# Where ScalarE, VectorE and GpSimd do their share of the SSD stages, and when the rotary tables are loaded

## The reference, cut to what matters

```python
xbc = jax.nn.silu(causal_dwconv(xbc, conv_w, conv_b))       # x, B, C of every group
cb = jnp.einsum('bclgn,bcsgn->bgcls', Cm, Bm)               # C B^T, shared by a group's 4 heads
y_diag = jnp.einsum('bgecls,bcsgep->bclgep',
                    cb[:, :, None] * jnp.exp(segsum(a_dt)), X)   # decay of every head, causal
y = y + xs * jnp.repeat(d_skip, SSD_HEAD_DIM)
y = (y * jax.nn.silu(z)).reshape(Bsz, T, SSD_GROUPS, SSD_INNER // SSD_GROUPS)
y = y * lax.rsqrt(jnp.mean(y * y, -1, keepdims=True) + EPS) # norm over a group's 256 channels
...
q = rotate_retnet(q, pos); k = rotate_retnet(k, pos) * RET_QK_DIM ** -0.5
scores = jnp.einsum('bclhd,bcshd->bhcls', q, k) * decay[None, :, None]
```

## Time and profile before

| | |
|---|---|
| median of three runs | 1806.04 us (1805.96 to 1806.24) |
| profiled execution | 1805.96 us, its span 1804.2 us (1.8 us lie outside the span) |
| PE busy | 1770.2 us, 98% of the span |
| DVE busy | 1204.9 us, 67% |
| ACT busy | 730.1 us, 40% |
| POOL busy | 16.7 us, 1% |

### The profile page before, as it was taken

How to read it: one execution, slowest core, us unless ns; L and a number is a source line. 1 busy time by engine, 2 the same in 40 slices (tenths; PEclk the granted TensorE clock), 3 DMA queues, 4 the chain that set the end, 5 groups by cost and what they waited for, 6 DMA issues and landing times.

```text
span 1804.2 us, 35149 instructions
## 1 busy us (share of the span) xinstructions
PE 1770.2 (98%) x13934; PEld 1686.2 (93%) x13934; DVE 1204.9 (67%) x1702; ACT 730.1 (40%) x1078; POOL 16.7 (1%) x58
## 2 busy tenths in 40 slices
PE   7999999999999999999999999999999999999996
PEld 7998899999999999999998888888989999999996
DVE  8788765545367877783344777777775788878323
ACT  5454441112143223222224777777774333322221
POOL 0000000000000000000000000000000000000000
PEclk9999999999999999999999999999999999999998
DMA  4322332222222322332222222221212222233221
GB/s 155 113 87 85 94 105 68 64 71 69 71 92 84 93 86 89 93 97 95 96 66 73 62 62 62 62 61 53 68 55 87 93 84 91 93 93 105 87 96 62
DMA packets 39936, 149.89 MB, mean 83 GB/s; under 512 B 4384, under 2 KB 5408, under 8 KB 39216
## 3 DMA queue, kind: packets, MB, share of 16 engines
q1 hardware_dynamic: 38672, 142.16, 25.1%
q10 hardware_dynamic: 1184, 6.60, 1.1%
HBM read 146.62 MB, written 2.13 MB: 82 GB/s over the span
## 4 chain that ended last, share of the span: by engine, by line
PE 86%; DVE 8%; ACT 3%; issue 2%; DVEq 0%; DMA 0%; ACTq 0%
PE gp L365 75%; PE small L411 4%; PE small L422 1%; DVE wlo L1121 1%; PE small L605 1%; PE small L615 1%; DVE xcv L1161 1%; DVE spb L1572 1%; PE small L464 1%; DVE gr L1161 1%; ACT lbuf L968 1%; DVE dec L1236 1%; ACT lbuf L971 0%; ACT whi L698 0%; DVE sp_lo L1596 0%
## 5 line engine op out<-in xcount | busy, mean ns | idle before, releaser
L365 PE MATMUL gp<-hn_hi,whi 128*128 128x264 f32 (+1 forms) x3216 | 662.3, 287 | 14.1 <-DVE wlo L1121 11.5
L365 PE MATMUL gp<-hn_hi,wlo 128*128 128x264 f32 (+1 forms) x3216 | 654.9, 285 | 0.0
L365 PE MATMUL gp<-hn_lo,whi 128*128 128x264 f32 (+1 forms) x3216 | 654.1, 285 | 0.0
L698 ACT ACTIVATE whi<-raw 128x1024 fp32r<-128x1024 f32 (+1 forms) x249 | 273.6, 1099 | 795.0 <-PE gp L365 794.4
L1121 DVE TENSOR_TENSOR wlo<-raw,whi 128x1024 fp32r<-128x1024 f32 (+1 forms) x249 | 317.5, 1275 | 336.5 <-ACT whi L698 336.2
L365 PEld LDWEIGHTS gp<-hn_hi,whi 128*128 128x128 f32 x3216 | 502.2, 190 | 18.9 <-DVE wlo L1121 12.0
L365 PEld LDWEIGHTS gp<-hn_lo,whi 128*128 128x128 f32 x3216 | 500.2, 189 | 0.0
L365 PEld LDWEIGHTS gp<-hn_hi,wlo 128*128 128x128 f32 x3216 | 499.4, 190 | 0.0
L365 PE MATMUL gp<-hid_lo,whi 128*128 128x264 f32 (+1 forms) x704 | 141.7, 283 | 0.0
L365 PE MATMUL gp<-hid_hi,wlo 128*128 128x264 f32 (+1 forms) x704 | 141.5, 282 | 0.0
L365 PE MATMUL gp<-hid_hi,whi 128*128 128x264 f32 (+1 forms) x704 | 141.4, 282 | 0.0
(11 more groups left out here) (234 smaller groups left out, 1732.6 us busy)
## 6 DMA issues: line engine op xcount, KB each, us to landing
raw<-in SPq DMA_DIRECT2D x217, 512.0 KB, 3.6
raw<-in SPq DMA_DIRECT2D x32, 704.0 KB, 4.1
cs_bc<-cs_scratch ACTq DMA_DIRECT2D x4, 1056.0 KB, 5.8
hT<-in SPq DMA_DIRECT2D x4, 528.0 KB, 7.5
out<-yT SPq DMA_DIRECT2D x4, 512.0 KB, 2.8
rdec<-in ACTq DMA_DIRECT2D x1, 1056.0 KB, 6.3
gw<-in SPq DMA_DIRECT2D x8, 128.0 KB, 3.4
rope<-in ACTq DMA_DIRECT2D x1, 528.0 KB, 3.7
```

Source lines behind the costliest of these rows:

```text
L365: ins = pe.matmul(gp[t.par][:, h, 0:half], wp[w.par][:, cols], rp[:, k0 + k, t0 + h * half:t0 + (h + 1) * half], start=first and k == 0 an ...
L698: act.activation(whi[w.par][:, 0:kt * P], raw[w.par][:, 0:kt * P], ACT.Copy).then_inc(hi_done, 1)
```

## The change

ACT: the Silu of B now waits for C's convolution too and is done with it in one instruction, ahead of those of x and z. The Ln and Exp of the norm (steps 6 and 7, now one step) come behind the stage's first `split_hi` and no longer around it. The decays of heads 2 and 3 come in slot 3, no longer in slot 4. DVE: `split_lo` comes ahead of the first two `args`; the other two `args` move from slot 3 to slot 2, ahead of `weigh_pair(g, 0)`, which itself goes to slot 3; the convolutions of tiles 2 and 3 move one slot back, to slots 4 and 5. POOL: the mask is put on each of the four `dec[h]`, behind the exponential, in place of the one `cbs`. The two tables lie elsewhere in memory, and ACT issues their loads in slot 7 of head 0 behind the last group's `norm_out`, where it issued them in slot 5 behind the last group's products.

```diff
             def ssd_silu(g):
-                act.wait_ge(conv_done, 4 * g + 3)
-                act.activation(xcv[:, 2, :], xcv[:, 2, :], ACT.Silu)
+                act.wait_ge(conv_done, 4 * (g + 1))
+                act.activation(xcv[:, 2:4, :], xcv[:, 2:4, :], ACT.Silu)
+                wait_count(act, ysum_done, g)
+                act.activation(xs[:], xcv[:, 0:2, :], ACT.Silu)
                 act.wait_ge(pair_free[(T_SSD + 4) % 2], (T_SSD + 4) // 2 + 1 + 3 * g)
                 act.activation(zc[:, 0, :], zc[:, 0, :], ACT.Silu)
-                wait_count(act, ysum_done, g)
-                act.activation(xs[:], xcv[:, 0:2, :], ACT.Silu)
-                act.wait_ge(conv_done, 4 * g + 4)
-                act.activation(xcv[:, 3, :], xcv[:, 3, :], ACT.Silu)
...
-                if step == 4:
+                if step == 3:
                     for h in range(2, 4):
                         decay(g, h)
...
-                if step == 7:
                     act.wait_ge(yln_done, g + 1)
                     act.activation(acc[:], acc[:], ACT.Exp, scale=-0.5).then_inc(yrs_done, 1)
...
             for c in range(8):          # ACT, retention head 0
...
-                if c == 5:
-
-                    act.wait_ge(y_done, 2 * SSD_GROUPS)
+                if c == 7:
+
+                    act.wait_ge(yout_done, SSD_GROUPS)
                     act.dma_start(rope[:], ...).then_inc(tab_in, 16)
                     act.dma_start(rdec[:], dec_h).then_inc(tab_in, 16)
...
             def weigh_pair(g, c):
-                    ve.wait_ge(e_done, HPG * g + h + 1)
-                    ve.wait_ge(cbm_done, g + 1)
+                    ve.wait_ge(es_done, HPG * g + h + 1)
+                    ve.wait_ge(cbs_done, g + 1)
...
                 if c == 0:              # DVE, ssd_slot
                     tile(-1)
+                    split_lo(w)
                     args(g, 0)
                     args(g, 1)
-                    split_lo(w)
...
                     conv_(1)
+                    args(g, 2)
+                    args(g, 3)
+                elif c == 3:
                     weigh_pair(g, 0)
-                elif c == 3:
                     split_lo(w)
                     tile(2)
-                    args(g, 2)
-                    args(g, 3)
-                    conv_(2)
                 elif c == 4:
                     split_lo(w)
                     weigh_pair(g, 1)
                     tile(3)
                     take(g, 0)
-                    conv_(3)
+                    conv_(2)
                 elif c == 5:
                     take(g, 1)
                     split_lo(w)
                     add_pair(g)
                     tile(4)
+                    conv_(3)
...
             with po.Fori(0, SSD_GROUPS) as g:
-                await_count(cbs_done, g + 1)
-                mask(cbs, cbm_done)
+                for h in range(HPG):
+                    await_count(e_done, HPG * g + h + 1, h)
+                    mask(dec[h], es_done)
```

More of the change, by code:

```diff
@@ L188, in build @@
             with scope() as s2:
+                rope = sb("rope", [P, 2, T], f32, s2)
+                rdec = sb("rdec", [P, RET_HEADS, T], f32, s2)
                 rq = sb("rq", [P, 2, T], f32, s2)
@@ L194, in build @@
                 o_tok = sb("o_tok", [P, NT, 256], f32, s2)
-                rope = sb("rope", [P, 2, T], f32, s2)
-                rdec = sb("rdec", [P, RET_HEADS, T], f32, s2)
                 stats = sb("stats", [P, NT, 6], f32, s2)
@@ L266, in build @@
         cb_done, cbs_done = sem("cb_done"), sem("cbs_done")
-        arg_done, e_done, cbm_done, m_done, y_done, yz_done = (
-            sem(n) for n in ("arg_done", "e_done", "cbm_done", "m_done", "y_done", "yz_done"))
+        arg_done, e_done, es_done, m_done, y_done, yz_done = (
+            sem(n) for n in ("arg_done", "e_done", "es_done", "m_done", "y_done", "yz_done"))
         ysq_done, ysum_done, ysums_done, yln_done, yrs_done, yout_done = (
@@ L807, in ssd_stage @@
                 for c in range(6):
-                    back = c == 0 and not (isinstance(g, int) and g < 2)
                     if c == 0:
                         ssd_small(g - 1, 0)
-                    if back:
-                        ssd_small(g - 2, 6)
                     split_hi(At(6, g, W_SSD + c + 1))
-                    if back:
-                        ssd_small(g - 2, 7)
                     if c > 0:
                         ssd_small(g - 1, c)
+                    if c == 0 and not (isinstance(g, int) and g < 2):
+                        ssd_small(g - 2, 6)
                     if c == 4:
@@ L841, in _ @@
             for c in range(8):
-                back = {0: SSD_GROUPS - 2, 6: SSD_GROUPS - 1}
                 if c == 0:
                     ssd_small(SSD_GROUPS - 1, 0)
-                if c in back:
-                    ssd_small(back[c], 6)
                 split_hi(At(8, 0, W_RET + c + 1))
-                if c in back:
-                    ssd_small(back[c], 7)
                 if 0 < c < 6:
                     ssd_small(SSD_GROUPS - 1, c)
-                if c == 5:
-                    act.wait_ge(y_done, 2 * SSD_GROUPS)
+                if c in (0, 6):
+                    ssd_small({0: SSD_GROUPS - 2, 6: SSD_GROUPS - 1}[c], 6)
+                if c == 7:
+                    act.wait_ge(yout_done, SSD_GROUPS)
                     act.dma_start(rope[:], cst_h[:, 5 * P:5 * P + 2 * T].rearrange("p (a t) -> p a t", a=2))\
```

## The result

The changed kernel took 1816.99 us (median of 4 runs, 1816.36 to 1817.84) against 1806.0 (4 runs, 1805.42 to 1806.24) on the same chip: ratio 1.0061, 95% interval 1.0044 to 1.0079. It is slower, as forecast, but by 11.0 us and not by 6.9, and outside the range of 1809.0 to 1816.0. Its profiled execution was faster than any of these four: 1813.89 us, with a span of 1812.0.

The account below looks back on a forecast made before the run. PE was taken to bound the kernel, busy for 1770.2 of 1804.2 us. 1805.96 + 2.3 (SSD stages) + 2.9 (tables) + 1.7 (clock) = 1812.9 us, range 1809.0 to 1816.0.

Parts of the forecast that it names:

- Term 1: SSD stages: PE delayed by a longer ACT and DVE chain and by masks, 1.6 + 0.7 = 2.3 us, bounds -1.2 and 4.3.
- Term 1, the lap: SSD stages: one lap through ACT and DVE around tile 3's convolution takes 9.3 + 19.4 + 19.1 = 47.8 us.
- Term 1, what waits behind it: Last group: C Bᵀ waits for x times dt, ready at 212.1 instead of starting at 210.53, so PE is 1.6 us late.
- Term 1, the masks: SSD stages: three more POOL masks beside DVE in each of three laps cost 0.6 to 2.7 us; 0.7 taken.
- Term 2: Retention head 0: DVE waits for the later table loads before the rotations, so PE's scores come 2.9 us later.
- Term 3: Ahead of the scores: PE's 2.5 us wait brings one half-clock stretch, 1.7 us; bounds 0 and 3.4.
- third rival: SSD stages: POOL and DVE get in each other's way, masks delay `weigh_pair(g, 1)`; 1815.2 us, 15 in 100.
- 1: SSD stages: PE's waits at tile 4 go and nothing replaces them; gain 1.2 us, 1804.8 us, 6 in 100.
- 2, the clock stays up: PE's clock does not fall, leaving the delays of SSD stages and tables alone; 1811.2 us, 20 in 100.
- 4: SSD stages' delay hidden (0) or `rdec` lands early (tables 1.5), no fall of the clock; 1807.5 us, 14 in 100.

Follow-up runs that it names:

- e3: The changed kernel with POOL's mask back on `cbs`, one a group: 1812.23 us, ratio 1.0036.
- e7: The kernel before with the changed DVE slots 2 to 5, ACT's Silus and decays; mask, Ln, tables and DVE's slot 0 as before: 1807.18 us, ratio 1.0013.
- e8: The kernel before with only Ln and Exp moved into one place behind the first high part: 1805.18 us, ratio 1.0.
- e1: The changed kernel once more, unaltered, for a second profile: 1814.14 us, ratio 1.0052.
- e6: The kernel before with only the masks moved to the four decays: 1809.86 us, ratio 1.0025.
- e10: e6 with the arguments and exponentials of heads 2 and 3 earlier, the other slots as before: 1808.77 us, ratio 1.0018.
- e5: The kernel before with only the tables moved and loaded in slot 7: 1808.47 us, ratio 1.0021.
- e2: The changed kernel with DVE's slots 2 to 5 as before: 1812.49 us, ratio 1.0039.
- e9: The changed kernel with DVE's wait for the tables moved just ahead of the rotations, behind the low part and evacuation: 1812.9 us, ratio 1.0043.
- e12: The kernel before with four more masks a group on a scratch tile that nobody waits for: 1806.4 us, ratio 1.0004.
- e4: The changed kernel with the tables' place and loads as before, in slot 5: 1810.1 us, ratio 1.0028.
- e11: The kernel before with `weigh_pair(g, 1)` and tile 4's evacuation each put ahead of its low part on DVE: 1805.24 us, ratio 0.9998.

## Why the prediction was right and where it failed

Four steps failed: the price of the masks, the instruction that C Bᵀ was said to wait for, the size of the wait for the tables, and the count of stretches at half clock.

**What bounds the kernel.** Right: PE's busy time is the same to 0.1 us in the first profile, and all that changed are its waits and where its clock fell.

**Term 1, the lap: right to 0.1 us.** Without the masks (e3) tile 3's convolution ended at 103.9, 151.7 and 199.5, where 103.6, 151.4 and 199.2 were forecast, and x times dt was ready at 212.1, as forecast. That it fits to the decimal is luck: the convolution ended 0.3 later, 0.2 of it start-up, and the way from there took 12.6 us, not 12.9. `zc` is no longer waited for.

**Term 1, what waits behind it: a step failed, 0.9 us.** "C Bᵀ waits for it. It began at 210.53: PE is 1.6 us late." It was not x times dt that came last. The transpositions wait for Ln, which reads the PSUM they write, and Ln ends 2.2 us behind the first high part in e3. In e3 they begin at 205.88, and with 7.0 us to C Bᵀ (the transpositions and a unit of 5.87) that makes 212.87: 2.5 late, not 1.6 (0.2 of it start-up). The working had the time of Ln in its lap (9.3 for ACT) and didn't ask which instruction of PE waits for it. e7 and e8 show that Ln's own move isn't the cost (0 alone, and 2.8 late at C Bᵀ without it): the Silus behind tile 3's convolution are.

**Term 1, the masks: the largest failure, 1.7 us.** "Three masks more in each of three laps are 0.6 to 2.7 us; I take 0.7, near the row." Measured: 2.4 at C Bᵀ (e1 against e3), and alone 4.95 (e6). The row is of a mask at a time when DVE did an evacuation and a convolution; beside DVE's products and low parts it is something else. In the changed kernel heads 2 and 3 have their masks where `weigh_pair(g, 0)` runs. Timelines of POOL and of DVE, changed kernel, in the same 10 us:

```profile
129.75 4.10 POOL L1728 TENSOR_TENSOR idle_g<-eps_col 128x1 f32<-128x1 f32 x1 [11.49 <-ACT dec L790]
133.80 2.15 POOL L1734 TENSOR_SCALAR_AFFINE_SELECT dec<-dec 128x128 f32<-128x128 f32 x5
135.92 0.19 POOL L1728 TENSOR_TENSOR idle_g<-eps_col 128x1 f32<-128x1 f32 x1
136.06 2.56 POOL L1734 TENSOR_SCALAR_AFFINE_SELECT dec<-dec 128x128 f32<-128x128 f32 x5
```

```profile
129.48 1.54 DVE L1227 TENSOR_TENSOR dec<-dec,cbs 128x1344 f32<-128x1344 f32 x1
...
131.03 1.54 DVE L1227 TENSOR_TENSOR dec<-dec,cbs 128x1344 f32<-128x1344 f32 x1
...
132.59 1.21 DVE L1112 TENSOR_TENSOR wlo<-raw,whi 128x1024 fp32r<-128x1024 f32 x1
...
138.66 1.56 DVE L1227 TENSOR_TENSOR dec<-dec,cbs 128x1344 f32<-128x1344 f32 x1 [0.89 <-POOL dec L1734]
```

POOL's tiny instruction on 128x1, 0.19 us elsewhere, stood from 129.75 to 133.85, that is through two products and the low part, until DVE fell idle at 133.80. The masks came behind it and took 2.15 and 2.56 us, and DVE then waited 0.89 for the second one. This is the third rival, in its place and nearly in its numbers ("take 2 us each", "waits 0.7 in each of two laps"). I had given it 15 in 100 and left it out of the sum. The Trainium skill's "SBUF — State Buffer", "SBUF: two separate sides", says that such DVE instructions and GpSimd's hold a shared pair of ports in turn. These rows agree that one engine stands while the other works, but "in turn" is not what they show: POOL got no turn between DVE's products and low part, and stood through all three. The sum should have gone by it.

The parts don't add up: at C Bᵀ the slots alone cost 2.8, the masks alone 4.95, both together 4.9. In e6 the arguments of heads 2 and 3 are later than in the changed kernel, and so the masks are later against their products; e10 shows that their place matters, but no run adds the parts up one by one.

**Term 2: right in mechanism, short in size.** "They end at 260.65 + 1.9 + 8.4", so 2.9 late. Measured from C Bᵀ to the scores: 3.6 alone (e5), 3.2 in e1 (8.0 less 4.85) and 4.3 in the profile of the changed kernel, 9.2 less 4.9. The load landed after 6.8, 6.3 and 7.4 us; the earlier trace rows had 6.3. The term is the landing less 3.1 in all three, and in e2 and e3 too (6.3 and 3.2, 6.7 and 3.6), where the forecast had the landing less 3.4. So 0.3 us was missing in the chain, and one transfer's time, seen once, was taken for a constant, while it moved over 1.1 us between executions. What stands behind the wait was as forecast: e9 gave back the 1.9 of low part and evacuation nearly whole (1.8).

**Term 3: the mechanism right, the count not.** "So I count one such stretch." PE's waits of 1.7 to 2.3 us are followed by half clock in some executions and not in others: at the scores in e1, e2 and e3 but neither in the first profile of the changed kernel nor in e5; in layer 1 in before, e1, e3, e8, e9, e10 and e12, and not in the changed kernel's first profile, e2, e4, e5, e6, e7 and e11. The waits of 2.24 to 2.26 for Ln are the same case: half clock behind one of them in the first profile, in e1 and in e4, and behind neither of the two in e9; of e6's two waits of 1.9 for `dec` one had it. The forecast took before's stretch in layer 1 as fixed; in the first profile of the changed kernel it was gone (1.7 won), and the one at 160 us cost nothing at the end, since the next lap on DVE and ACT was the later one (the transpositions behind it began at 208.27, and at 208.35 in e4, which had no stretch there).

**The sum once more, for the profiled execution:** 1805.96 + 4.9 (term 1, 2.3 forecast) + 4.3 (term 2, 2.9 forecast) - 1.7 (clock, +1.7 forecast) = 1813.5, measured 1813.89. The forecast of 1812.9 came within 1 us of it only because two terms that were too small stood against a third that was too large.

**The median is 3.1 us above that execution.** With two stretches that count, as in e1, and a load of 7.4 us, the sum gives 1802.5 + 9.2 + 3.4 + 1.8 = 1816.9, the median. The timed runs left no traces, so this is inferred, not shown; e1's profile shows two such stretches with the same code. Why the five executions of e1 have a median of only 1814.14 stays open. It lies inside the forecast's range, but that would have been luck: the same steps are wrong in e1's profile too (4.85 at C Bᵀ, 3.2 and two stretches).

**The rivals.** 1 fell: nothing was won at tile 4. 2, the clock stays up, held for the scores in one profile of two, with the other terms larger. 3 was the mechanism that was missing. 4 fell: term 1 was 4.9.

## What to carry to other kernels

Where a chain through one engine grows, walk along the critical engine's own order and ask of each piece what it waits for; the first one that is late decides, not the last. Price a GpSimd instruction by a row in which DVE does what it will do beside it, and take a row of a single transfer as a sample. Where a wait may bring half clock in some executions, the range has to hold each number of stretches, those of the kernel before too.

## What the runs showed of the hardware

- A mask of five `affine_select` took 1.17 us beside an evacuation by DVE and 4.44 beside a convolution, a low part and a product (e12); the longest of all took 5.17 (e10, at 85.49). The smallest instruction of POOL went from 0.19 to 4.10 us beside products with two inputs. DVE is held up less often: an instruction of 0.54 us took 1.43 twice (e10).
- Between the start and the last column sums all stretches at half clock lasted 3.4 us, in the 14 profiles, and cost 1.7 where PE was the bound. They stood behind waits of PE of 1.7 to 2.3 us. With the same instructions and the same wait (2.20 us at the scores) one execution had one and another not.
- A load of 1056 KB on ACT's queue landed after 6.2 to 7.4 us in 14 profiles of this case; in the six with the late load (the changed kernel, e1, e2, e3, e5, e9) after 6.3 to 7.4.
